# GLA and pooling trunk: one block for projection, attention and mixing, the last gates in another buffer, W_out's first part after tile 1's

## The chip, the core and the metric

The kernel runs on one core of one Trainium2 chip. The metric is the device time of one execution in microseconds (us), median of several runs. The core has five engines with instruction streams of their own: PE (TensorE: matmuls into PSUM banks), ACT (ScalarE), DVE (VectorE), POOL (GpSimd) and SP (SyncE, which here issues nearly all DMAs). They order each other by semaphores: an instruction raises one when it is done, another waits for a value. Sixteen DMA engines move data between HBM and SBUF.

## What is computed

Two layers over x of shape (1, 2048, 1024), all in float32. The first is a gated linear attention in chunks of 64 rows with 4 heads:

```python
h = x @ w_in
q, k, v, g, lr = split(h)
gk = log_sigmoid(lr @ w_gk + b_gk) / 16
bcum = cumsum(gk, within chunk)
qe, ke, kd = q * exp(bcum), k * exp(-bcum), k * exp(b_last - bcum)
o = tril(qe @ ke.T) @ v + qe @ S_prev       # S: state carried from chunk to chunk
o = rmsnorm(o) * norm_w * silu(g)
x = layernorm(ALPHA * x + o @ w_out)
```

The second layer projects x to a pooled branch and a gate, takes causal means over 2, 4, 8 and 16 rows, multiplies by a matrix for each group and by the gate, projects back, and ends in the same residual and norm.

## The kernel before

Every large product is made of three PE matmuls of rounded halves (L213 to L215): an operand is copied by ACT to a rounded "hi", and DVE subtracts it from the raw value for a "lo". So each new operand costs one ACT and one DVE instruction before PE can use it.

The program has three stages. `prepare` folds weights and has its own block. `project` (L543) computes q, k, v and the gates in 24 steps of 7 products each; its instructions stand in a second block (L731), one stream for each engine. Attention (`attend_and_norm`, L1484) and mixing (`pool_mix_and_out`, L2144) share a third block (L3035). Where a block ends, all engines meet: none begins the next block before all have ended this one. After the second block POOL clears the semaphores of the projection (L1479), whose numbers the mixing uses again.

Some work of attention is already written into the end of the projection's streams: the scores, outputs and key-value product of tile 0 on PE (`first_scores`, `first_outputs`, `first_kv`), tile 0's hi and lo parts, and on SP the loads of tile 0 and tile 1 and the first two of four loads of W_out (1 MB each). The last things that each engine does in the projection's block are: PE tile 0's key-value product; ACT `last_silu` and the copies of the last turned keys (`copy_keys`, L1162) into `kn_last`; DVE the decays of tiles and `norm_of` the last gates (L1422); SP four stores of these gates (`store_gates`, L793), each after `norm_of`.

Attention works on 16 tiles of 128 rows. In the third block SP first stores `kn_last` (two DMAs, L1694), loads W_out's last two parts (L1697), the gates g of tiles 0 and 1, x of tile 0, and then in step 0 q, k2, kn and v of tile 2 (L189), the norm's parameters and x of tile 1. Each step t of the other engines:

- ACT (L1917): the rounded sum, Ln and Exp for the RMS norm of tile t-1, the rounded gated output, then `kv_parts` of tile t+1 (L1865: kn_hi and v_hi, which wait for all four loads of that tile), then the square of tile t's output. In steps 0 to 2 parts of W_out (`w_parts`, L1873, 16 in all, each 128x512) are spread between these: part 0 ahead of `kv_parts` in step 0, parts 1 and 2 behind it, 3 and 4 at the step's end; in step 1 parts 5 to 7 behind `kv_parts` and 8 to 11 at the end. Part n needs W_out's load (n mod 8) // 2.
- DVE (L2088): masks of the scores, W_out's part 0 in step 0 (L2093), `advance` (the state: a copy in step 0), the gated product of tile t-1 (two multiplications, the second by the loaded g), o_lo, `kv_parts` of tile t+1 (L2045: q times the decay, kn_lo, v_lo), further parts of W_out, the sums of squares, the residual of tile t-2. In step 0 DVE waits ahead of `kv_parts` of tile 1 until the gates are stored (L2048), since the buffer of v_lo of tile 1 overlaps that of the last gates, `g_main` (L589).
- PE (L1821): scores of tile t; after the state and `kv_parts` the key-value product of the tile (12 matmuls of 128x256); the product with W_out of tile t-2 (from step 2 on, 24 matmuls of 128x512 in each half, with the two matmuls of the RMS mean after the first six); the outputs of tile t.

Of the kernel before, what the change touches and what calls it, by code (L numbers as in the profile page):

```python
# [4 lines left out]
F32 = mybir.dt.float32  # L5
F32R = mybir.dt.float32r
I32 = mybir.dt.int32
ALU = mybir.AluOpType
# [3 lines left out]
P = 128  # L12
# [530 lines left out]
def project(nc, p, a, last_copy, last_store, ahead):  # L543
# [44 lines left out]
    g_at = p.at = p.w_end  # L588
    g_main = p.place("h_g_main", [P, 4, BLK])  # L589
# [4 lines left out]
    chunk_end = p.place("h_chunk_end", [P, HALF_CHUNKS])  # L594
    assert p.at <= SBUF_END
# [17 lines left out]
    held = []  # L613

    def sem(name):
        held.append(nc.alloc_semaphore("h_" + name))
        return held[-1]

# [6 lines left out]
    (columns, w_summed, x_hi_done, x_lo_done, product_mm, seeded, p5_copied, u2_copied, c11_copied, c21_copied,  # L625
     u3_added, c12_added, rows_loaded, x_turned, x_copied, x_stored, x_summed, terms_stored, rank_loaded, rank_hi, rank_lo, rank_mm,
     rank_rounded, rank_ready, gk_loaded, gk_hi, gk_lo, gk_mm, ln_done, chain, scanned, ends_read, q_exp, exps_ready, q_done,
     turned, kn_copied, silu, normed) = (
        sem(n) for n in (
            "columns", "w_summed", "x_hi_done", "x_lo_done", "product_mm", "seeded", "p5_copied",  # L630
            "u2_copied", "c11_copied", "c21_copied", "u3_added", "c12_added", "rows_loaded", "x_turned", "x_copied", "x_stored", "x_summed", "terms_stored",
            "rank_loaded", "rank_hi", "rank_lo", "rank_mm", "rank_rounded", "rank_ready", "gk_loaded", "gk_hi", "gk_lo",
            "gk_mm", "ln_done", "chain", "scanned", "ends_read", "q_exp", "exps_ready", "q_done", "turned", "kn_copied",
            "silu", "normed"))
# [96 lines left out]
    with nc.Block() as block:  # L731

        @block.sync
        def _(sp):
            def load_pair(i):

                if i < V_STEPS:
                    p.load_x_pair(sp, raws[i % 2], i)
                    return
                for b in range(2):  # L740
                    sp.dma_start(raws[i % 2][:, b * KT:(b + 1) * KT, :], w_src[:, :, column(i, b):column(i, b) + P]
                                 ).then_inc(pair_loaded[i % 2], DMA)

            def load_x(e, n):

                sp.wait_ge(product_mm, 7 * (e * EPOCH - 1) + n + 1)
                sp.dma_start(x_raw[ORDER[n]][:], p.x_in[e - 1, (0, 1, 3, 7, 4, 5, 6)[ORDER[n] - 1]]
                             ).then_inc(x_loaded[n], DMA)

            def load_gk(m):  # L750

                h = m % HEADS
                if m:
                    sp.wait_ge(gk_lo, m)
                for r in range(RANK_ROWS // GATE_RANK):
                    sp.dma_start(w_gk_raw[r * GATE_RANK:(r + 1) * GATE_RANK, :],
                                 a["gla_w_gk"][0][:, h * DK:(h + 1) * DK]).then_inc(gk_loaded, DMA)

            def load_rows(u):

                if u > KT:
                    sp.wait_ge(x_turned, u - KT)
                first = p.x_tile(u) * P
                sp.dma_start(rows[:], a["x"][0][first:first + P, :]).then_inc(rows_loaded, DMA)

            def store_x(u):

                sp.wait_ge(x_copied, u - KT + 1)
                half, c, b = u // KT, u % KT // 2, u % 2
                sp.dma_start(p.x_in[half, 2 * b:2 * b + 2, :, c, :].rearrange("q p n -> p q n"),  # L770
                             x_out[:].rearrange("p (q k) t -> p q (k t)", q=2)).then_inc(x_stored, DMA)

            def store_x_terms(i):
                sp.wait_ge(x_summed, 4 * (i + 1))
                sp.dma_start(p.x_in[i // HALF_K, 4:8, :, i % HALF_K, :].rearrange("q p n -> p q n"), terms[:]
                             ).then_inc(terms_stored, DMA)

            def store_v(i, b):
                if b:
                    sp.wait_ge(u3_added, i + 1)  # L780
                    sp.wait_ge(c21_copied, i + 1)
                else:
                    sp.wait_ge(c11_copied, i + 1)
                    sp.wait_ge(c12_added, i + 1)
                sp.dma_start(p.v_tiles[p.x_tile(2 * i + b)], v_out[i % 2][:, b, :]).then_inc(v_stored[i % 2], DMA)

            def store(scratch, m, col, n, src, stored):

                first = (m // HEADS * 2 + n) * HALF_K
                sp.dma_start(scratch[first:first + HALF_K, :, col * P:(col + 1) * P].rearrange("t p c -> p t c"),  # L790
                             src.rearrange("p (t c) -> p t c", c=P)).then_inc(stored, DMA)

            def store_gates(m):  # L793
                for j in range(2):
                    sp.wait_ge(normed, 2 * m + j + 1)
                    for n in range(2):
                        store(p.g_tiles, m, m % HEADS * 2 + j, n, gates(m)[:, 2 * j + n, :],
                              g_stored[ALT if m % HEADS == 0 else MAIN])

            def store_q(m):  # L800
                for n in range(2):
                    sp.wait_ge(q_done, 2 * m + n + 1)
                    store(p.q_tiles, m, m % HEADS, n, e_q[:, n * BLK:(n + 1) * BLK], q_stored)

            def store_k(m, n):
                sp.wait_ge(k_done[n], m + 1)
                store(p.k2_tiles, m, m % HEADS, n, k2_of(m)[:, n, :], k_stored)

            def store_kn(m):
                for n in range(2):  # L810
                    sp.wait_ge(kn_copied, 2 * m + n + 1)
                    store(p.kn_tiles, m, m % HEADS, n, kn_of(m)[:, n, :], kn_stored)

            def load_columns():
                with nc.allow_non_contiguous_dma(reason="small parameter vectors as columns"):
                    for dst, src in ((p.b_gk, a["gla_b_gk"][0].rearrange("(h d) -> d h", d=P)),
                                     (p.norm_w, a["gla_norm_w"][0].rearrange("(j d) -> d j", d=P)),
                                     (p.b_grp, a["pool_b_grp"][0].rearrange("g (m d) -> d (g m)", d=P)),
                                     (p.scale, a["pool_scale"][0].rearrange("(m d) -> d m", d=P))):
                        sp.dma_start(dst[:], src).then_inc(columns, DMA)  # L820

            load_rows(KT)
            last_store(sp)
            for s in range(2):
                sp.wait_ge(p.x_in_stored[s], NT // 4 * DMA)
            load_pair(1)
            load_gk(0)
            with nc.allow_non_contiguous_dma(reason="16 columns of the gates' first factor"):
                sp.dma_start(rank_raw[:], w_src[:, :, 2 * KD + 2 * VD:2 * KD + 2 * VD + GATE_RANK]
                             ).then_inc(rank_loaded, DMA)  # L830
            for i in range(STEPS):
                e = i // EPOCH + 1
                for n in range(-1, PRODUCTS - 1):
                    if n == -1 and 1 <= i <= V_STEPS:
                        store_v(i - 1, 1)
                    if n == -1 and i and i % EPOCH == 0:
                        load_x(e - 1, PRODUCTS - 1)
                    if n >= 0 and i % EPOCH == EPOCH - 1 and i + 1 < STEPS:
                        if n == 0:
                            sp.wait_ge(terms_stored, HALF_K * e * DMA)  # L840
                        load_x(e, n)
                    if n == 0 and i + 2 < STEPS:
                        sp.wait_ge(w_lo_done, parts_to(i, PRODUCTS - 1))
                        sp.wait_ge(w_hi_done, PRODUCTS * (i + 1))
                        if i:
                            sp.wait_ge(w_summed, 4 * i)
                        if i < V_STEPS:
                            sp.wait_ge(x_summed, 4 * (i + 1))
                        if HALF_K <= i + 2 < V_STEPS:
                            sp.wait_ge(x_stored, 2 * (i + 3 - HALF_K) * DMA)  # L850
                        load_pair(i + 2)
                    if i == 0 and n == 0:
                        store_x_terms(0)
                    if i < HALF_K and n in (2, 5):
                        u = KT + 2 * i + n // 5
                        if u + 1 < NT:
                            load_rows(u + 1)
                        if n == 2:
                            store_x(u)
                    if 1 <= i <= HALF_K and n == -1:  # L860
                        store_x(KT + 2 * i - 1)
# [2215 lines left out]
```

## Time and profile before

| | |
|---|---|
| median of 3 runs | 1888.73 us (1887.55 to 1889.65) |
| the profiled execution's own time | 1888.95 us |
| its span, first to last instruction | 1887.4 us |
| mean granted clock of PE | 0.993 |
| PE / PEld / DVE / ACT / POOL busy | 97% / 80% / 72% / 45% / 35% |
| DMA | 342.83 MB, mean 182 GB/s |

The page gives shares over the whole span, in which stages with different limits are mixed. What the change touches lies between 615 and 675 us of the span, so the rows further down come from that stretch: what each engine does there, what ended its idle time, when DMAs land, how busy the DMA engines are and which clock PE was granted. Times in the rows are us from the start of the span. Weight loads overlap matmuls, so matmuls of 128x512 that take 0.39 us each start 0.23 us apart.

### The profile page before, as it was taken

The numbers are of one execution on the slowest core, as the hardware profiler recorded it, in microseconds if no ns is written. First come the engines' busy times: TensorE is split into PE (matmuls) and PEld (weight loads), VectorE is DVE, ScalarE is ACT, GpSimd is POOL, SyncE is SP. The second block draws the span as 40 slices with busy tenths as digits, with TensorE's granted clock in tenths as the row PEclk, the third lists the DMA queues.
The fourth block names the chain that finished last, engine by engine and source line by source line (L and its number), as shares of the span: only waits on it lengthen the run. The fifth ranks groups of instructions, "written<-read, shape, count | busy, mean of one in ns | idle before, by whom it ended". The sixth has DMA issues, their size and how long they took to land.

```text
span 1887.4 us, 24159 instructions
## 1 busy us (share of the span) xinstructions
PE 1840.1 (97%) x8554; PEld 1510.0 (80%) x8554; DVE 1365.1 (72%) x1647; ACT 848.7 (45%) x1308; POOL 659.1 (35%) x460
## 2 busy tenths in 40 slices
PE   9999999999999799999989999999999999999997
PEld 8878886888788688888768888878888887887885
DVE  3565566667666688787786768668899978447997
ACT  4554335656555544444444444354343444224231
POOL 0432232323231000244445655315576634223330
PEclk9999999999999899999999999999999999999998
DMA  9967764438344854675734443243456436647542
GB/s 308 317 214 247 220 208 162 124 100 292 79 136 115 310 168 150 215 250 195 264 120 133 157 148 134 98 156 123 157 187 203 148 121 234 234 145 267 179 145 101
DMA packets 256068, 342.83 MB, mean 182 GB/s; under 512 B 19024, under 2 KB 184656, under 8 KB 251344
## 3 DMA queue, kind: packets, MB, share of 16 engines
q1 hardware_dynamic: 253264, 333.97, 53.0%
q0 software_dynamic: 2688, 7.34, 1.2%
q8 instruction: 68, 1.11, 0.2%
q14 instruction: 48, 0.39, 0.1%
HBM read 221.73 MB, written 119.54 MB: 181 GB/s over the span
## 4 chain that ended last, share of the span: by engine, by line
PE 56%; DVE 5%; issue 2%; DMA 1%; ACT 1%; POOL 1%; SPq 0%; DVEq 0%; ACTq 0%; POOLq 0%
PE banks L215 17%; PE banks L213 17%; PE banks L214 17%; PE banks L1813 1%; PE banks L1817 1%; DVE m_w_lo L2799 1%; DVE m_x_lo L2813 1%; PE banks L2582 1%; DMA v<-v_tiles 1%; DMA m_ahead<-x_terms 1%; PE banks L1611 0%; PE banks L2542 0%; ACT m_x_hi L2619 0%; DVE a_stats L2040 0%; PE banks L1804 0%
## 5 line engine op out<-in xcount | busy, mean ns | idle before, releaser
L213 PE MATMUL banks<-m_x_hi,m_w_hi 128*128 128x512 f32 x1312 | 515.2, 393 | 10.2 <-DVE m_z L2874 4.4
L215 PE MATMUL banks<-m_x_hi,m_w_lo 128*128 128x512 f32 x1312 | 513.8, 392 | 0.0
L214 PE MATMUL banks<-m_x_lo,m_w_hi 128*128 128x512 f32 x1312 | 513.2, 391 | 0.0
L213 PEld LDWEIGHTS banks<-m_x_hi,m_w_hi 128*128 128x128 f32 x1312 | 247.0, 188 | 66.7 <-issue 8.3
L214 PEld LDWEIGHTS banks<-m_x_lo,m_w_hi 128*128 128x128 f32 x1312 | 246.9, 188 | 53.2 <-issue 0.7
L215 PEld LDWEIGHTS banks<-m_x_hi,m_w_lo 128*128 128x128 f32 x1312 | 246.7, 188 | 52.2
L213 PE MATMUL banks<-b_hi,h_w_hi 128*128 128x512 f32 x656 | 258.1, 393 | 4.0 <-issue 3.0
L214 PE MATMUL banks<-b_lo,h_w_hi 128*128 128x512 f32 x656 | 256.5, 391 | 0.0
L215 PE MATMUL banks<-b_hi,h_w_lo 128*128 128x512 f32 x656 | 256.4, 391 | 0.0
L2606 ACT ACTIVATE m_w_hi<-m_s 128x512 fp32r<-128x512 f32 x182 | 114.4, 629 | 204.1 <-PE banks L215 176.3
L2799 DVE TENSOR_TENSOR m_w_lo<-m_s,m_w_hi 128x512 fp32r<-128x512 f32 x182 | 161.2, 890 | 31.4 <-ACT m_w_hi L2606 30.3
L213 PEld LDWEIGHTS banks<-b_hi,h_w_hi 128*128 128x128 f32 x656 | 123.6, 188 | 31.2 <-issue 5.8
L215 PEld LDWEIGHTS banks<-b_hi,h_w_lo 128*128 128x128 f32 x656 | 123.6, 188 | 25.8
L214 PEld LDWEIGHTS banks<-b_lo,h_w_hi 128*128 128x128 f32 x656 | 123.7, 189 | 25.1
L1290 DVE TENSOR_TENSOR h_w_lo<-h_s,h_w_hi 128x512 fp32r<-128x512 f32 x93 | 70.2, 757 | 66.9 <-ACT h_w_hi L1023 66.0
L213 PE MATMUL banks<-a_w_hi,a_o_hi 128*128 128x512 f32 x256 | 101.6, 397 | 0.4 <-DVE a_res L2037 0.4
L215 PE MATMUL banks<-a_w_hi,a_o_lo 128*128 128x512 f32 x256 | 100.1, 391 | 0.0
L214 PE MATMUL banks<-a_w_lo,a_o_hi 128*128 128x512 f32 x256 | 100.0, 391 | 0.0
L1978 POOL TENSOR_TENSOR m_stage_t<-m_stage_b,m_stage_a 128x256 f32<-128x256 f32 x8 | 6.0, 747 | 257.3 <-ACT m_stage_b L1908 257.3
L2751 POOL TENSOR_TENSOR m_s<-pair_raw 128x512 f32<-128x512 f32 x24 | 45.6, 1901 | 127.2 <-PE banks L2582 81.1
L1023 ACT ACTIVATE h_w_hi<-h_s 128x512 fp32r<-128x512 f32 x93 | 58.3, 628 | 56.1 <-PE banks L215 50.3
L2799 DVE TENSOR_TENSOR m_w_lo<-m_pair_raw,m_w_hi 128x512 fp32r<-128x512 f32 x69 | 64.4, 934 | 24.7 <-ACT m_w_hi L2606 24.4
(281 smaller groups left out, 3365.3 us busy)
## 6 DMA issues: line engine op xcount, KB each, us to landing
b_raw<-x_in SPq DMA_DIRECT2D x14, 1024.0 KB, 10.6
m_x_raw<-x_terms SPq DMA_DIRECT2D x9, 1024.0 KB, 8.4
p_in<-in_pool_w_in SPq DMA_DIRECT2D x32, 256.0 KB, 5.2
w_fused<-p_out SPq DMA_DIRECT2D x32, 256.0 KB, 3.6
x_in<-h_terms SPq DMA_DIRECT2D x8, 1024.0 KB, 4.3
v_tiles<-h_v_out SPq DMA_DIRECT2D x16, 512.0 KB, 5.0
in_raw<-in_gla_w_in SPq DMA_DIRECT2D x16, 512.0 KB, 6.1
h_raw<-in_gla_w_in SPq DMA_DIRECT2D x16, 512.0 KB, 6.0
```

The costliest lines, as they stand in the source:

```text
L213: nc.tensor.matmul(out, a_hi, b_hi, start=first, stop=False, skip_group_check=True)
L214: nc.tensor.matmul(out, a_hi, b_lo, start=False, stop=False, skip_group_check=True)
L215: return nc.tensor.matmul(out, a_lo, b_hi, start=False, stop=last, skip_group_check=True)
L1023: nc.scalar.activation(parts[ORDER[n]][:], weights(i, ORDER[n]), ACT.Copy).then_inc(w_hi_done, 1)
L1290: nc.vector.tensor_tensor(w_lo[j][:], weights(i, j), w_hi[j][:].bitcast(F32), ALU.subtract).then_inc(w_lo_done, 1)
L1813: nc.tensor.matmul(o_ps[:, j * P:(j + 1) * P], v[s][:, j * P:(j + 1) * P], scores[s][:, h * P:(h + 1) * P], start=j == 4 * b, stop=False, ...
L1817: last = nc.tensor.matmul(o_ps[:, j * P:(j + 1) * P], state[s][:, j * P:(j + 1) * P], q[s][:, j // 2, P:2 * P], start=False, stop=True, sk ...
L2582: last = nc.tensor.matmul(bank(i, j), weights(set_of(i), j)[:, k, :], x_raw[j][:, k, :], start=opens and k == 0, stop=k == HALF_K - 1, ski ...
L2606: nc.scalar.activation(w_hi[ORDER[n]][:], weights(s, ORDER[n]), ACT.Copy).then_inc(w_hi_done, 1)
L2751: nc.gpsimd.tensor_tensor(s3[:], a11, a21, ALU.subtract).then_inc(w_summed, 1)
L2799: nc.vector.tensor_tensor(w_lo[j][:], weights(s, j), w_hi[j][:].bitcast(F32), ALU.subtract).then_inc(w_lo_done, 1)
L2813: nc.vector.tensor_tensor(x_lo[j][:], loaded(e, n), x_hi[j][:].bitcast(F32), ALU.subtract).then_inc(x_lo_done, 1)
```

## The change

The projection's streams become functions like those of attention and mixing, and `kernel` calls them at the head of the third block; the second block and POOL's clearing of semaphores are gone. Since all semaphores now live at once, some are shared by projection and mixing (`x_loaded`, `p5_copied`, `u2_copied`, and `ln_loaded` by attention and mixing), whose waits add what the earlier stage has counted. SP waits for the copies of `kn_last` before it stores them, which the meeting had ordered. `g_main` moves to the place of the staging buffers of step 8 and later, so DVE's wait on the stored gates goes. In step 0 DVE does `kv_parts` of tile 1 ahead of `advance` and of all parts of W_out, and ACT ahead of part 0, which both now do later in the step. Without the indentation, and without the renamed semaphores:

```diff
-def project(nc, p, a, last_copy, last_store, ahead):
+def project(nc, p, a, phase, last_copy, last_store, ahead):
...
-    g_at = p.at = p.w_end
-    g_main = p.place("h_g_main", [P, 4, BLK])
+    p.at = p.w_end
     u2 = p.place("h_u2", [P, BLK])
...
     chunk_end = p.place("h_chunk_end", [P, HALF_CHUNKS])
+    assert p.at <= p.rows_at + 2 * D * 4
+    g_at = p.at = p.rows_at + 2 * D * 4
+    g_main = p.place("h_g_main", [P, 4, BLK])
...
-    with nc.Block() as block:
-
-        @block.sync
-        def _(sp):
+    def sync(sp):
...
-    for s in held:
-        nc.gpsimd.sem_clear(s)
-        nc.release_semaphore(s)
+
+    return sync, tensor, scalar, gpsimd, vector
...
         for n in range(2):
             first, col = (2 + n) * HALF_K, HEADS - 1
+            sp.wait_ge(p.kn_copied, 2 * (2 * HEADS - 1) + n + 1)
             sp.dma_start(p.kn_tiles[first:first + HALF_K, :, col * P:(col + 1) * P].rearrange("t p c -> p t c"),
...
-            w_parts(t, {0: (0, 1), 2: (12, 16)})
+            w_parts(t, {2: (12, 16)})
             if has_next(t):
                 kv_parts(t + 1, 1 - s, pair + s, lag + 1)
-            w_parts(t, {0: (1, 3), 1: (5, 8)})
+            w_parts(t, {1: (5, 8)})
...
-            w_parts(t, {0: (3, 5), 1: (8, 12)})
+            w_parts(t, {0: (0, 5), 1: (8, 12)})
...
         def kv_parts(t, s):
 
-            if isinstance(t, int) and t == 1:
-                dve.wait_ge(p.g_stored[0], 6 * 4 * DMA)
...
-            w_parts(t, {0: (0, 1)})
+            if first(t):
+                kv_parts(1, 1)
...
-            if has_next(t):
+            if has_next(t) and not first(t):
                 kv_parts(t + 1, 1 - s)
...
-            w_parts(t, {0: (1, 3)})
+            w_parts(t, {0: (0, 3)})
...
             with nc.Block() as block:
 
                 @block.sync
                 def _(sp):
+                    produce[0](sp)
                     mix[0](sp, *attend[0](sp, load_first, load_second))
```

The other four streams get their `produce` call in the same way.

## Rows read from the trace of the kernel before

**Rows 1.** The page: busy us of each engine, share of the span, instructions.

```profile
PE 1840.1 (97%) x8554; PEld 1510.0 (80%) x8554; DVE 1365.1 (72%) x1647; ACT 848.7 (45%) x1308; POOL 659.1 (35%) x460
```

**Rows 2.** Timeline of PE: start, duration, line, [idle before, what ended it].

```profile
630.84 1.13 PE L1611 MATMUL banks<-q,k 128*128 128x128 f32 x8 [0.48 <-PEq L731]
637.01 0.55 PE L213 MATMUL banks<-a_v_hi,a_kn_hi 128*128 128x256 f32 x1 [5.05 <-DVE a_v_lo L2054]
...
643.55 1.32 PE L1813 MATMUL banks<-a_scores,v 128*128 128x128 f32 x8 [2.79 <-DVE a_gated L2013]
...
651.21 0.35 PE L213 MATMUL banks<-a_v_hi,a_kn_hi 128*128 128x256 f32 x1 [1.32 <-DVE a_v_lo L2054]
...
654.96 0.47 PE L1761 MATMUL banks<-a_sum_hi,mean_w 128*128 128x512 f32 x1 [0.71 <-issue]
```

**Rows 3.** Timeline of ACT.

```profile
626.83 1.09 ACT L1169 ACTIVATE h_kn_last<-banks 128x512 f32<-128x512 f32 x2
630.65 1.28 ACT L1910 ACT_TABLE_LOAD   x1 [2.73 <-PEq L731]
...
633.00 1.04 ACT L1871 ACTIVATE a_v_hi<-v 128x1024 fp32r<-128x1024 f32 x1
```

**Rows 4.** Timeline of DVE.

```profile
626.97 1.42 DVE L1428 TENSOR_SCALAR h_g_main<-h_g_main,norm_w 128x1024 f32<-128x1024 f32 x2 [1.55 <-ACT h_g_main L1203]
...
632.70 0.69 DVE L2063 TENSOR_TENSOR a_w_lo<-a_w_raw,a_w_hi 128x512 fp32r<-128x512 f32 x1 [4.32 <-ACT a_w_hi L1879]
...
635.65 1.22 DVE L2054 TENSOR_TENSOR a_v_lo<-v,a_v_hi 128x1024 fp32r<-128x1024 f32 x1
...
643.44 1.23 DVE L2018 TENSOR_TENSOR a_gated<-a_gated,a_g 128x1024 f32<-128x1024 f32 x1
```

**Rows 5.** The chain in order of time: start, duration, what.

```profile
637.54 10.41 DMA v<-v_tiles
647.97 0.64 ACT a_kn_hi L1870
```

**Rows 6.** DMA issues by narrow windows: KB, us to landing; at 623.6, 631.9, 633.7, 637.5.

```profile
v<-v_tiles SPq DMA_DIRECT2D x1, 512.0 KB, 4.7
...
a_w_raw<-in_gla_w_out SPq DMA_DIRECT2D x1, 1024.0 KB, 6.1
...
a_g<-g_tiles SPq DMA_DIRECT2D x1, 512.0 KB, 8.2
...
v<-v_tiles SPq DMA_DIRECT2D x1, 512.0 KB, 10.4
```

**Rows 7.** Windows: us, PE, PEld, DVE, ACT, POOL busy, PE clock, DMA share, GB/s.

```profile
628.00:629.00 1.00, 1.00 (x11) 1.00 (x10) 0.39 (x1) 0.00 (x0) 0.00 (x0) 1.00 0.32 89
629.00:630.00 1.00, 1.00 (x11) 1.00 (x10) 0.00 (x0) 0.00 (x0) 0.00 (x0) 1.00 1.00 279
...
634.00:635.00 1.00, 0.00 (x0) 0.00 (x0) 1.00 (x2) 1.00 (x4) 0.00 (x0) 0.56 0.87 194
635.00:636.00 1.00, 0.00 (x0) 0.00 (x0) 1.00 (x3) 0.99 (x2) 0.00 (x0) 0.50 1.02 401
...
656.00:658.00 2.00, 2.00 (x10) 1.65 (x9) 1.56 (x4) 1.43 (x3) 0.00 (x0) 1.00 0.05 17
```

**Rows 8.** Timeline of SP's issues of DMAs.

```profile
627.75 2.30 SPq L790 DMA_DIRECT2D g_tiles<-h_g_main  x4
630.64 1.24 SPq L1694 DMA_DIRECT2D kn_tiles<-h_kn_last  x2
631.93 1.71 SPq L204 DMA_DIRECT2D a_w_raw<-in_gla_w_out  x2
```

**Rows 9.** Timeline of PE after another pause, later in the kernel.

```profile
954.51 0.47 PE L213 MATMUL banks<-m_x_hi,m_w_hi 128*128 128x512 f32 x1 [4.44 <-DVE m_z L2874]
...
955.12 0.63 PE L215 MATMUL banks<-m_x_hi,m_w_lo 128*128 128x512 f32 x1
...
958.10 0.53 PE L213 MATMUL banks<-m_x_hi,m_w_hi 128*128 128x512 f32 x1
```

More of the change, by code:

```diff
@@ L612, in project @@
     p.g_main, p.kn_last = g_main, kn_last
[L613 to L617, printed above, removed]
+    sem = lambda name: phase.enter_context(nc.semaphore("h_" + name))
     pair_loaded, g_stored = p.in_loaded, p.g_stored
@@ new lines, in gpsimd, with sums_read, weight_sums @@
+    def gpsimd(pool):
+        def sums_read(i, j):
+            if native(i - 1, POS[j]):
+                pool.wait_ge(w_hi_done, PRODUCTS * (i - 1) + POS[j] + 1)
+            else:
+                pool.wait_ge(w_lo_done, parts_to(i - 1, POS[j]))
+        def weight_sums(i):
+            a11, a12, a21, a22 = weights(i, 1), weights(i, 2), second_row(i), weights(i, 4)
+            pool.wait_ge(pair_loaded[i % 2], 2 * (i // 2 + 1) * DMA)
+            sums_read(i, 5)
+            nc.gpsimd.tensor_tensor(s1[:], a21, a22, ALU.add).then_inc(w_summed, 1)
+            pool.wait_ge(w_summed, 4 * (i - 1) + 1)
+            sums_read(i, 6)
+            nc.gpsimd.tensor_tensor(s2[:], s1[:], a11, ALU.subtract).then_inc(w_summed, 1)
+            sums_read(i, 7)
+            nc.gpsimd.tensor_tensor(s3[:], a11, a21, ALU.subtract).then_inc(w_summed, 1)
+            sums_read(i, 3)
+            pool.wait_ge(w_summed, 4 * (i - 1) + 2)
+            nc.gpsimd.tensor_tensor(s4[:], a12, s2[:], ALU.subtract).then_inc(w_summed, 1)
+        for i in range(1, STEPS):
+            weight_sums(i)
@@ L2235, in pool_mix_and_out @@
     (w_summed, w_hi_done, w_lo_done, product_mm,
[L2236 removed]
+     seeded, c11_copied, u3_added, c12_added, silu_n1, silu_n2, chain, padded, pooled, mixed,
      stage_turned, stage_copied, stage_sum, stage_stored, x_hi_done, x_lo_done, out_added, stats_done, moments_done,
[L2238 removed]
+     rstd_done, normed_mid, normed, out_rows_loaded, out_summed, out_terms_stored) = (
         sem(n) for n in (
[L2240 removed]
+            "w_summed", "w_hi_done", "w_lo_done", "product_mm", "seeded", "c11_copied", "u3_added",
             "c12_added", "silu_n1", "silu_n2", "chain", "padded", "pooled", "mixed", "stage_turned", "stage_copied",
             "stage_sum", "stage_stored", "x_hi_done", "x_lo_done", "out_added", "stats_done", "moments_done", "rstd_done",
[L2243 to L2244 removed]
+            "normed_mid", "normed", "out_rows_loaded", "out_summed", "out_terms_stored"))
+    p5_copied, u2_copied, x_loaded, ln_loaded = p.p5_copied, p.u2_copied, p.x_loaded, p.ln_loaded
+    STEPS_BEFORE, TURNS_BEFORE, NORMS_BEFORE = 3 * (NT // 2), 2, 1
     res_loaded, out_stored = ([sem(f"{n}{s}") for s in range(4)] for n in ("res_loaded", "out_stored"))
@@ L2555, in free @@
             elif j == 7:
-                pe.wait_ge(*((u2_copied, i + 1) if i < MIX else added(i, 2)))
+                pe.wait_ge(*((u2_copied, STEPS_BEFORE + i + 1) if i < MIX else added(i, 2)))
             elif j == 3:
-                pe.wait_ge(*((p5_copied, i + 1) if i < MIX else added(i, 1)))
+                pe.wait_ge(*((p5_copied, STEPS_BEFORE + i + 1) if i < MIX else added(i, 1)))
             elif j == 4:
@@ L2566, in operands @@
                 pe.wait_ge(*weights_ready(s, j))
-                pe.wait_ge(x_loaded[n], (e + 1) * DMA)
+                pe.wait_ge(x_loaded[n], (TURNS_BEFORE + e + 1) * DMA)
                 return
@@ L2615, in turn_hi @@
             j = ORDER[n]
-            act.wait_ge(x_loaded[n], (e + 1) * DMA)
+            act.wait_ge(x_loaded[n], (TURNS_BEFORE + e + 1) * DMA)
             if e:
@@ L2916, in norm_end @@
             n, r = 2 * (o - SECOND) + b, res[res_at(o)][:, b, :]
-            dve.wait_ge(ln_loaded, 2 * DMA)
+            dve.wait_ge(ln_loaded, 2 * (NORMS_BEFORE + 1) * DMA)
             dve.wait_ge(moments_done, n + 1)
@@ L3032, in gla_pool_trunk @@
             attend, ahead = attend_and_norm(nc, p, a, phase)
-            project(nc, p, a, *prepare(nc, p, a), ahead)
+            produce = project(nc, p, a, phase, *prepare(nc, p, a), ahead)
             load_first, load_second, *mix = pool_mix_and_out(nc, p, a, out_dram, phase)
@@ L3042, in _ @@
                 def _(pe):
+                    produce[1](pe)
                     mix[1](pe, *attend[1](pe))
@@ L3050, in _ @@
                 def _(pool):
+                    produce[3](pool)
                     attend[3](pool)
```

1274 lines of the change are left out of this document (624 added, 650 removed).

## Prediction

> **What bounds the kernel now.** The page first: PE is busy for 97% of the span [rows 1]. So a change is worth only what it takes out of PE's idle time, or out of a stretch where something else sets the pace. The change touches one such stretch, some 20 us around the end of the projection, so I read that stretch engine by engine.
>
> PE first [rows 2]. It works without a gap up to the key-value product of tile 0, idles 0.48 for the meeting, does the scores of tile 1, and then idles 5.05 us until DVE has tile 1's v_lo. Later it idles 2.79, 1.32 and 0.71. These are the prizes. ACT and DVE say why the 5.05 exist [rows 3, 4]: ACT is done with the projection at 626.83 + 1.09 = 627.92 and DVE at 626.97 + 1.42 = 628.39, but both begin attention behind the meeting, ACT with a table load at 630.65 and DVE with a part of W_out at 632.70; tile 1's keys and values come after those.
>
> Then the chain in order of time, which tells what I would have missed by looking at engines alone [rows 5]. For 10.41 us, up to 648, it is no engine's work but the load of tile 2's v. ACT starts tile 2 when that load lands, and PE's product of tile 2 at 651.21 follows through DVE's v_lo [rows 2]. From there on PE has little idle time, and the change alters no order in that part. So the question of this change is one number: when does tile 2's v land?
>
> Is that load late because SP issues it late, or because the DMA engines are full? By the landings, W_out's third part takes 6.1 us, the first gates 8.2, tile 2's v 10.4, while tile 1's v, issued alone at 623.6, took 4.7 [rows 6]. The later in SP's order, the longer the wait: a queue that grows. The windows agree: the DMA share is 0.32 at 628, then about 1.0 in each microsecond, with one dip to 0.87 at 634, until it falls to 0.05 after 656 [rows 7]. So the stretch from 629 to 648 is bound by the bytes in flight, in SP's order: 1 MB of gates stored, 0.5 of keys, 2 of W_out, 1 of gates, 0.5 of x, 0.75 of q, k2 and kn, 0.5 of v, together 6.25 MB or 6.55 million bytes, in 19 us: 345 GB/s.
>
> **The change part by part.**
>
> *The meeting goes.* PE gains 0.48; ACT can start 630.65 - 627.92 = 2.7 us earlier, DVE 632.70 - 628.39 = 4.3 [rows 2 to 4]. SP ended its last stores of gates at 627.75 + 2.30 = 630.05 and went on at 630.64: it gains 0.59 [rows 8]. Its new wait (both halves of the last kn copied) is on ACT's copies that end at 627.92 [rows 3], 2 us before SP gets there, so it costs nothing; behind it in SP's order stand the stores of kn, W_out's last parts and all loads of tile 2, so a late copy would delay them one for one. POOL has no work here.
>
> *The gates' other buffer* changes where 1 MB is read from, not when, and lets DVE drop its wait on the stored gates. That wait ended nothing before: DVE's work from 632.70 to v_lo at 635.65 has no gap. With tile 1 moved up it would have bound, since the stores are issued until 630.05 [rows 4, 8].
>
> *Tile 1 ahead of W_out.* New times, from the durations above. ACT: 627.92, table load 1.28 gives 629.2, kn_hi 0.6 gives 629.8, v_hi 1.04 gives 630.8; tile 1's v has landed at 623.6 + 4.7 = 628.3 [rows 3, 5, 6]. DVE: q and kn_lo 0.6 each from 629.8, v_lo 1.2 to 632.2, then the copy of the state, as large as v_lo, to 633.4 [rows 4]. PE needs both, so tile 1's product starts at 633.4 instead of 637.01: 3.6 us earlier. Next is W_out: the moved part 0 (one of 16 on each of two engines, 0.6 and 0.7 us) changes places with tile 1's parts and is hidden by the waits that follow. But ACT's part 4 needs W_out's third load, 631.93 + 6.1 = 638.0 by its issue and landing, and the gates of tile 0 land at 633.7 + 8.2 = 641.9, where DVE used them at 643.44 [rows 4, 6, 8]. So of the 3.6 us DVE's gated product keeps 1.5. After it ACT and DVE stand at tile 2's v, which their program order puts ahead of W_out's parts 5 to 7, so these can't fill the gap.
>
> *What is late next* is thus tile 2's v. SP comes to it 0.59 us earlier at most: one end is -0.59. The other end is 0: the queue holds the same bytes in the same order, and a queue that is never empty lands its last byte at the same time. A loss is excluded on this term, since nothing new stands ahead of that load. The row at 634 tells between the ends: the DMA engines were idle for 0.13 us there, and moved 194 GB/s where the next microsecond had 401, so between a tenth and half of a microsecond was lost where SP's stores end and W_out's loads begin [rows 7]. An earlier SP closes this hole and no more. I take -0.3.
>
> *PE's clock.* The 5.05 us of idle brought the granted clock down: 0.56 at 634, 0.50 at 635 [rows 7]. Before tile 2's product at 651.21 PE idled only 1.32 us, behind 6.3 us of work (outputs of tile 1 from 643.55, 5.4 us at a slow pace, then scores), and that product ran at full pace [rows 2]. With the change the outputs start at about 641 (W_out's part 4, two short ACT steps and DVE's first gated product after 638.0) and are over by 646.5; then PE waits for tile 2's v, does 0.9 us of scores at 647.7 and waits 2.3 more. Little work and much idle, and then the stretch where PE is full. What does the trace say of the price? After 4.44 us of idle at 954.51, seven products started between 955.12 and 958.10, 0.43 apart; at the usual 0.23 they would have taken 1.4 us less [rows 9]. The bounds here: 0 if the clock stays up; at most half clock all the way to the mean of tile 2, which is twelve 128x256 products (0.1 each), six 128x512 and the two of the mean (0.2 each by rows 9), 2.8 us, of which PE's wait of 0.71 before that mean covers a part [rows 2]: +2.1. I take +0.6, nearest to the fall of rows 9: 1.4 less the 0.71. The Trainium skill, "TensorE: Matmul & The Clock Gate", section "HAM oscillation — how this bites in real kernels", says that a wait for DMA between tiles lets the clock gate throttle again, so that each next tile starts slow. The trace bears this out in part: the pauses of 5.05 and 4.44 us were followed by half clock, that of 1.32 was not. Where it held in full, the time would be that of the second rival below.
>
> *Sum.* Against the profiled execution's own 1888.95 (span 1887.4, the rest lies around it): -0.3 + 0.6 = +0.3. That execution is 0.2 above the median 1888.73, so about 1889.0. The 3.6 us that tile 1 wins are real, and are given back in the wait for tile 2's v.
>
> **The rivals.**
>
> *The whole wait comes back (faster).* If the 10.41 us of tile 2's v were SP's lateness and not the queue's, tile 1's gain would pass on: 3.6 us at the product and 0.48 of the meeting, up to the full 5.05, hence 1883.7 to 1884.7. For it: tile 2's v is the last of eleven issues that SP makes one after another from 630.64 on [rows 8]. Against: the share of 1.0 [rows 7], and that SP moves by 0.59 only.
>
> *PE meets tile 2 at half clock (slower).* Place: 651.21. Price: the far bound above, +2.1, with no help from the load: 1890.8. It decides when PE's idle before that product grows beyond the 1.32 that it stood and is not made up by work in between; the idle of 2.79 at 643.55 is the nearest larger one [rows 2]. To be slower by a margin that can be measured it would have to lose 3.8 + 0.7 us, some 9 us at half clock, three times the 3 us of rows 9.
>
> *It doesn't do what it says.* If DVE or ACT still stand at a wait that the meeting hid (tile 1's loads, the stored keys), tile 1 starts as late as now, and the time is that of before, 1888.7.
>
> **How the numbers follow.** Chances: forecast (tile 2's v sets the end, some clock lost) 0.74; the whole wait 0.10; half clock at tile 2 0.12; no effect 0.04. The forecast's ends, -0.59 and +1.2, with the 1 us by which the runs before spread give 1887.1 to 1890.9. Taking in the half clock, and leaving out the whole wait: 1886.9 to 1891.5. About 0.2%, 3.8 us, is what a measurement of this kernel can tell from no change. Faster by more: the whole wait, 0.10. Slower by more: the far part of the half clock, 0.05. The rest, 0.85, is within it.
>
> **What would show it.** In the changed kernel: ACT's table load near 628; PE's idle before tile 1's product shrunk from 5.05 to about 2; tile 1's v_lo at 631; a DMA share of 1.0 without the dip near 634; ACT idle before tile 2's kn_hi, released by the load of v, until 647.4 to 648; PE's product of tile 2 within 0.6 us of 651.2. The clock near 651 tells the third term. I am wrong if tile 2's v lands before 645, or if the DMA share falls below 1 between 630 and 648.

## The result, and the profile after

The changed kernel took 1890.83 us (median of 12 runs, 1889.13 to 1894.31), the kernel before, beside it, 1887.62 (12 runs, 1886.61 to 1889.65): a ratio of 1.0019, 95% interval 1.0010 to 1.0028. Measured a second time, in another series, it took 1888.24 against 1888.00, ratio 1.0004 (0.9995 to 1.0013). So the change gives nothing, and perhaps costs a little; 1889.0 was forecast. The profiled execution took 1890.05, its span is 1888.3, and the page's busy times are those of [rows 1] but for 3.5 us at most:

```profile
PE 1839.9 (97%) x8554; PEld 1508.5 (80%) x8554; DVE 1368.6 (72%) x1647; ACT 849.2 (45%) x1308; POOL 662.1 (35%) x460
```

All stands earlier or later here by what the stages before it took. So times below are often given from the first store of the last gates, SP's first row, which is 627.75 in the kernel before [rows 8]. SP's timeline after (start, duration):

```profile
626.60 2.31 SPq L786 DMA_DIRECT2D g_tiles<-h_g_main  x4
628.96 1.78 SPq L1686 DMA_DIRECT2D kn_tiles<-h_kn_last  x2
630.78 1.72 SPq L204 DMA_DIRECT2D a_w_raw<-in_gla_w_out  x2
...
636.62 1.20 SPq L186 DMA_DIRECT2D v<-v_tiles  x1
```

SP goes on 0.05 us after the stores of the gates, where it stood 0.59 before [rows 8]; but the two stores of keys now take 1.78 to issue in place of 1.24, and at W_out SP is level again: 630.78 - 626.60 = 4.18, as 631.93 - 627.75 = 4.18 before. Tile 1 did what was forecast. ACT and DVE:

```profile
626.79 1.28 ACT L1902 ACT_TABLE_LOAD   x1
...
637.10 0.63 ACT L1871 ACTIVATE a_w_hi<-a_w_raw 128x512 fp32r<-128x512 f32 x1 [1.34 <-DMA a_w_raw<-in_gla_w_out]
...
648.23 0.63 ACT L1862 ACTIVATE a_kn_hi<-kn 128x512 fp32r<-128x512 f32 x1 [4.90 <-DMA v<-v_tiles]
```

```profile
630.06 1.22 DVE L2044 TENSOR_TENSOR a_v_lo<-v,a_v_hi 128x1024 fp32r<-128x1024 f32 x1
...
641.01 1.23 DVE L2010 TENSOR_TENSOR a_gated<-a_gated,a_g 128x1024 f32<-128x1024 f32 x1 [0.79 <-DMA a_g<-g_tiles]
...
648.89 0.69 DVE L2042 TENSOR_TENSOR q<-q,a_tile_decay 128x512 f32<-128x512 f32 x1 [4.30 <-ACT a_kn_hi L1862]
```

The table load follows the copies of the last keys at once (it waited 2.73, [rows 3]). Then the gain is spent piece by piece, each time in a wait for a load: 1.34 us for W_out's third part, 0.79 for the gates, and 4.90 for tile 2's v, where DVE waits 4.30 in its turn. PE shows the same:

```profile
632.47 0.39 PE L213 MATMUL banks<-a_v_hi,a_kn_hi 128*128 128x256 f32 x1 [2.36 <-DVE a_state L1991]
...
640.37 2.04 PE L1805 MATMUL banks<-a_scores,v 128*128 128x128 f32 x8 [5.18 <-DVE a_gated L2005]
...
648.25 1.16 PE L1602 MATMUL banks<-q,k 128*128 128x128 f32 x8 [2.04 <-DMA v<-v_tiles]
...
651.47 0.55 PE L213 MATMUL banks<-a_v_hi,a_kn_hi 128*128 128x256 f32 x1 [2.06 <-DVE a_v_lo L2044]
...
673.58 0.50 PE L1753 MATMUL banks<-a_sum_hi,mean_w 128*128 128x512 f32 x1 [0.27 <-DVE a_sum_lo L2075]
```

Tile 1's product begins 5.87 us after the gates' store (9.26 before): 3.4 earlier. Tile 2's begins 24.87 after it, 23.46 before: 1.4 later. The chain in order of time names the load between them:

```profile
636.62 11.59 DMA v<-v_tiles
648.23 0.64 ACT a_kn_hi L1862
```

11.59 us where it was 10.41 [rows 5], though the DMA share is 0.99 or more in each microsecond from 635 to the landing. Windows (the columns of [rows 7]) show this, and the clock:

```profile
634.00:635.00 1.00, 0.68 (x4) 0.30 (x2) 1.00 (x3) 1.00 (x3) 0.00 (x0) 1.00 0.86 328
635.00:636.00 1.00, 0.19 (x1) 0.00 (x0) 1.00 (x3) 0.76 (x2) 0.00 (x0) 1.00 0.99 401
...
647.00:648.00 1.00, 0.00 (x0) 0.00 (x0) 0.00 (x0) 0.00 (x0) 0.00 (x0) 1.00 1.02 410
...
652.00:653.00 1.00, 1.00 (x7) 1.00 (x6) 1.00 (x2) 0.27 (x1) 0.00 (x0) 0.50 1.08 346
```

At 647 no engine does anything at all, and the DMA engines move 410 GB/s: the stage is bound by bytes in flight. From 651.5 to 654.9 PE works at granted clock 0.50, where the kernel before had 1.00:

```profile
652.00:653.00 1.00, 1.00 (x10) 0.95 (x9) 1.00 (x3) 0.02 (x1) 0.00 (x0) 1.00 1.06 347
```

SP issues the same transfers in the same order in both kernels, so a transfer that differs must be one that SP does not issue. The list of DMA queues has it, in windows of 2 us: after at 644 to 646, ahead of v's landing at 648.2, and before at 647 to 649, around its landing at 647.95 (number of packets, MB, share of 16 engines):

```profile
q8 instruction: 1, 0.02, 3.4%
```

The row is word for word the same in both kernels; only its place differs. One packet of 16 KB fetches instructions, and 3.4% of 16 engines for 2 us is 1.09 us on one engine. It can be placed more closely: between the landing of tile 2's kn and that of its v, which SP issues next. From the issue of kn (SP's rows, before and after) and its time to landing (the same row in both):

```profile
636.65 0.84 SPq L182 DMA_DIRECT2D kn<-kn_tiles  x1
635.71 0.87 SPq L182 DMA_DIRECT2D kn<-kn_tiles  x1
kn<-kn_tiles SPq DMA_DIRECT2D x1, 256.0 KB, 10.0
```

kn has landed at 646.65 before and at 645.71 after, v 1.3 us later before and 2.5 later after. So of the 1.4 us that v comes later (from the gates' store), some 1.2 arise between these two landings, where the fetch lies; 0.2 are there already at kn.

Where these few us go between the two profiled executions, from the rows above and [rows 8]: the stages before the gates' store -1.15 (626.60 against 627.75, work that the change does not touch; in the thirteen traces of this case the place lies between 624.8 and 629.0); from there to tile 3's mean +1.58 (673.58 - 626.60 = 46.98; before, 673.15 - 627.75 = 45.40); behind it +0.47; in all the +0.9 by which the spans differ. The row of before, from its chain:

```profile
673.15 0.51 PE banks L1761
```

### The profile page after: what moved, and what is told of

The parts are those of the page before. It is cut to its first block, busy times and chain, and to the rows that moved or that the text cites. A ratio compares the mean times of both kernels' runs of the same rounds, so it can differ in the third digit from the quotient of the medians.

```text
span 1888.3 us, 24097 instructions
## 1 busy us (share of the span) xinstructions
PE 1839.9 (97%) x8554; PEld 1508.5 (80%) x8554; DVE 1368.6 (72%) x1647; ACT 849.2 (45%) x1308; POOL 662.1 (35%) x460
## 4 chain that ended last, share of the span: by engine, by line
PE 79%; DVE 5%; issue 3%; DMA 3%; ACT 2%; SPq 1%; POOL 1%; DVEq 0%; ACTq 0%; POOLq 0%
PE banks L213 24%; PE banks L215 24%; PE banks L214 24%; PE banks L1805 1%; PE banks L1809 1%; DVE m_w_lo L2791 1%; PE banks L954 1%; DVE m_x_lo L2805 1%; DMA m_x_raw<-w_terms 1%; PE banks L932 1%; ACT m_x_hi L2611 1%; DMA v<-v_tiles 1%; DMA m_ahead<-x_terms 1%; DMA b_raw<-x_in 1%; PE banks L1602 0%
## 5 line engine op out<-in xcount | busy, mean ns | idle before, releaser
L2791 DVE TENSOR_TENSOR m_w_lo<-pair_raw,m_w_hi 128x512 fp32r<-128x512 f32 x72 | 65.2, 906 | 26.0 <-ACT m_w_hi L2598 25.5
```

Source lines behind the costliest of these rows:

```text
L2791: nc.vector.tensor_tensor(w_lo[j][:], weights(s, j), w_hi[j][:].bitcast(F32), ALU.subtract).then_inc(w_lo_done, 1)
```

## The experiments

Three theories. Q: the stage ends when tile 2's v lands; what the change wins stops there, and an instruction fetch that PE, running ahead in tile 1, now brings in front of that landing makes it later still. C: PE's clock loses the time. R: what differs lies in the rest of the kernel, and from run to run. The measures, all worked out as above, in us from the first store of the last gates:

| kernel | time, beside before | v of tile 2 lands | fetch begins | mean of tile 2 | mean of tile 3 |
|---|---|---|---|---|---|
| before | | 20.20 | 19.8 | 27.21 | 45.40 |
| changed | 1890.83, 1887.62 | 21.61 | 18.5 | 29.27 | 46.98 |
| changed, again | 1888.24, 1888.00 | 21.54 | 18.2 | 29.50 | 47.21 |
| parts moved, meeting kept | 1887.65, 1888.00 | 20.11 | 20.1 | 27.12 | 45.31 |
| one block, parts not moved | 1890.36, 1888.08 | 21.52 | 18.7 | 29.20 | 46.91 |
| outputs held | 1888.18, 1888.08 | 20.50 | 24.7 | 28.35 | 46.06 |
| waits for PE | 1892.98, 1888.00 | 21.76 | 19.4 | 28.78 | 46.97 |
| three products | 1889.33, 1888.08 | 22.15 | 18.8 | 29.16 | 47.35 |
| tile 2 first | 1883.77, 1888.00 | 14.01 | 17.4 | 23.19 | 41.16 |
| tile 2 first, meeting kept | 1885.71, 1888.08 | 13.85 | 19.6 | 25.48 | 43.66 |
| tile 2 first, again | 1883.89, 1888.35 | 13.84 | 17.3 | 22.77 | 40.95 |

**The changed kernel again**, with no edit.

> The changed kernel once more, for a second trace and a second set of times. Theory Q (the DMA queue and the instruction fetch in it set tile 2's start): the load of tile 2's v lands again 21 to 22 us after the first store of the last gates (20.2 before, 21.6 in the first trace of the changed kernel), with an instruction-fetch DMA between 640 and 648 us; the loss up to the PE product of tile 2 is again 1 to 2 us, and the time is 2 to 4 us above the kernel before. Theory C (PE's clock is the loss): the product of tile 2 starts as early as before against the gates' stores, and the loss stands in slow products after it, other in each trace. Theory R (the loss is spread over the mixing): the two kernels differ by more behind 700 us than ahead of it.

Ratio 1.0004 (0.9995 to 1.0013). The landing at 21.54 and tile 3's mean at 47.21 repeat the first trace: the stage loses 1.6 to 1.8 us, 0.09% of the kernel, each time; of the 2 to 4 us that were expected in the time, 0.2 came. The rest of the first measurement's 0.19% did not repeat. Behind tile 3's mean the two traces are 0.5 us longer and 0.5 shorter than before: what theory R looks at is scatter in these traces, and shows no loss of the change.

**Parts moved, meeting kept.** The kernel before with the other buffer and tile 1 ahead of W_out, but two blocks:

```diff
-    g_at = p.at = p.w_end
-    g_main = p.place("h_g_main", [P, 4, BLK])
+    p.at = p.w_end
...
+    g_at = p.at = p.rows_at + 2 * D * 4
+    g_main = p.place("h_g_main", [P, 4, BLK])
...
-            w_parts(t, {0: (0, 1)})
+            if first(t):
+                kv_parts(1, 1)
```

> The kernel before with its two blocks and the meeting, but with the gates in the other buffer and tile 1's parts ahead of W_out's: one part of the change alone. Theory Q: tile 2's v comes as in the kernel before, so the time is that of before within 1 us (1887 to 1889), and the fetch of instructions lies as in before. Theory C: PE's idle before tile 2 grows as in the changed kernel, since tile 1 starts 1 to 2 us earlier, and 1 to 3 us are lost: 1889 to 1891. Theory R: as before.

Ratio 1.0001 (0.9992 to 1.0010), v at 20.11. Moving the parts alone costs nothing and wins nothing. Its chain row:

```profile
635.05 10.40 DMA v<-v_tiles
```

**One block, parts not moved.** The changed kernel with the parts of tile 1 behind W_out's part 0, as before:

```diff
-            if first(t):
-                kv_parts(1, 1)
+            w_parts(t, {0: (0, 1)})
...
-            if has_next(t) and not first(t):
+            if has_next(t):
                 kv_parts(t + 1, 1 - s)
```

> The changed kernel with W_out's part 0 ahead of tile 1 again and the state's copy ahead of tile 1's parts: the one block and the other buffer alone. Theory Q: tile 1 still starts some 3 us earlier than before and PE runs ahead of the fetch's old place, so v lands 21.3 to 21.7 us after the first store of the gates and the time is that of the changed kernel within 1 us, 1888 to 1889.5. If the moved parts were the cause of the loss: v lands at 20.2 and the time is that of before.

Ratio 1.0010 (1.0001 to 1.0019). v lands at 21.52 and the load takes 11.32 us: the loss of the load is there in full without the moved parts (the time, 1890.36, is 0.9 above what was expected). It comes with the meeting's end, and so does PE's running ahead: the fetch begins at 18.7, as in the changed kernel.

```profile
635.10 11.32 DMA v<-v_tiles
```

**Outputs held.** If the fetch is the cause, v must land early again when PE reaches that place later. PE's second half of tile 1's outputs waits until tile 2's four loads have landed; no DMA that the kernel issues is touched.

```diff
-        def outputs(s):
+        def outputs(s, hold=False):
...
             for b in range(2):
+                if hold and b:
+                    pe.wait_ge(in_loaded[1 - s], 2 * p.QKV_LOADS * DMA)
...
-                outputs(s)
+                outputs(s, isinstance(t, int) and t == 1)
```

> The changed kernel, but PE does the second half of tile 1's outputs only when tile 2's four loads have landed. PE then comes later to the place in its stream at which the next 16 KB of its instructions are fetched (18.1 and 18.5 us after the first store of the gates in the two traces of the changed kernel, ahead of tile 2's v). Theory Q with the fetch as the cause: the fetch comes after that landing, v lands 20.1 to 20.5 us after the first store of the gates instead of 21.5 to 21.6, and the time falls by 1 to 2 us against the changed kernel; PE's 1.8 us of held outputs and 0.9 of scores fit into the 3.2 us that ACT and DVE need after the landing. If the fetch isn't the cause: v lands at 21.5 to 21.6 again and the time stays or grows by up to 1 us.

The fetch begins at 24.7, behind the landing, and v lands at 20.50, 1.2 us behind kn, its load again as long as before:

```profile
634.88 10.44 DMA v<-v_tiles
```

Of the 1.3 to 1.4 us, 1.1 are back, by an edit to PE alone. This is the run that shows Q's second half. Ratio 1.0008 (0.9999 to 1.0017): what the load gives back, the held products spend in part, so tile 3's mean gains only 0.9 to 46.06, and the 1 to 2 us expected in the time do not show (1888.18; the changed kernel 1890.83 and 1888.24).

**Waits for PE.** Meant to move the fetch by other means, some 200 waits that are long met, spread over PE's products in the projection, so that its instruction blocks fall elsewhere:

```diff
             last.then_inc(product_mm, 1)
+            for _ in range(2 if i < 5 else 1):
+                pe.wait_ge(w_hi_done, 1)
```

> The changed kernel with some 200 waits that are already met, added behind products of the projection on PE, so that the fetches of PE's instructions (16 KB each, about 256 instructions apart) fall elsewhere: no longer between 628 and 648 us while the DMA engines are full, but near 623 and 651. Theory Q with the fetch as the cause: tile 2's v lands about 1.2 us earlier against the gates' stores (20.2 to 20.5 us after the first), and the time falls by 1 to 2 us, to 1889. If the fetch isn't the cause: it lands as before, 21.6 us after, and the time stays. The waits themselves cost under 1 us.

Only 61 of them became instructions of their own, and the fetch moved from 18.5 to 19.4, still 2.3 us ahead of the landing at 21.76, so the run does not do what it was meant to. The kernel was slower, 1.0029 (1.0019 to 1.0038), by something outside the stage that stays open. But its trace shows which measure to trust. The load of v took 10.44 us here, just as without a fetch ahead of it, but SP issued it 1.3 later (11.33 us after the gates' store, against 10.01), so the length of a load alone doesn't tell what delayed it. The time from kn's landing to v's does: it is 1.9 here, 1.8 to 2.5 in all five traces with the fetch well ahead of v's landing (the two of the changed kernel, one block, waits for PE, three products), and 1.2 to 1.3 in the other eight.

**Three products.** Theory C by itself: three products of 128x512 that nobody reads, on PE, two behind tile 1's outputs and one behind tile 2's scores, to keep the clock up.

```diff
+        def filler(count):
+            for _ in range(count):
+                nc.tensor.matmul(y_ps[0], p.ident[:], p.mask[:].rearrange("p h c -> p (h c)"), start=True, stop=True)
...
                 scores_of(s)
+                if isinstance(t, int) and t == LAG:
+                    filler(1)
...
                 outputs(s)
+                if isinstance(t, int) and t == 1:
+                    filler(2)
```

> The changed kernel with three 128x512 products of constants on PE whose result nobody reads: two behind the outputs of tile 1, one behind the scores of tile 2, to keep PE at work while it waits for tile 2's v. Theory C: the clock stays at 1.00 from 648 to 655, tile 2's product runs at its full pace, and the mean of tile 2 starts 0.4 to 0.8 us earlier against the gates' stores (28.5 to 28.9 us after the first instead of 29.3 to 29.5). Under both theories v lands where it did, 21.5 us after, and the time falls by at most 0.8 us, within what can be told from no change.

The clock stayed up at tile 2 (the windows of this kernel; the changed one had 0.50):

```profile
652.00:653.00 1.00, 1.00 (x11) 1.00 (x10) 1.00 (x2) 0.27 (x1) 0.00 (x0) 1.00 1.09 390
```

From v's landing to tile 2's mean it took 7.01 us, as in the kernel before (27.21 - 20.20 = 7.01); the changed one took 29.27 - 21.61 = 7.66, and 7.96 the second time. So the clock costs 0.65 to 0.95 there. But in this trace v landed 0.5 later, and tile 3's mean is no earlier; the ratio is 1.0010 (1.0001 to 1.0019). The clock's price is shown; that removing it speeds the kernel up is not.

**Tile 2 first.** Q's first half. SP issues W_out's third part, the gates of tile 0 and then all of tile 2, and only then W_out's last part, the keys' stores, the gates of tile 1 and x: 2.5 MB less ahead of v.

```diff
+        p.load_out_rows(sp, 2)
+        load_g(0, 0)
+        sp.wait_ge(o_mm, 1)
+        p.load_qkv(sp, 2, 0)
+        p.load_out_rows(sp, 3)
         for n in range(2):
...
-        for n in (2, 3):
-            p.load_out_rows(sp, n)
-        load_g(0, 0)
...
-            if not (static and t + 2 >= NT):
+            if not (static and (t == 0 or t + 2 >= NT)):
```

> The changed kernel with SP's order altered: W_out's third part, the gates of tile 0, then tile 2's q, k2, kn and v, and only then W_out's fourth part, the stores of the last kn, the gates of tile 1 and x. 2.5 MB that stood ahead of tile 2's v go behind it. Theory Q: tile 2's v lands 5 to 7 us earlier, at about 641 to 643, the PE product of tile 2 starts at 645 to 647 instead of 651.5, and the time falls by 3.5 to 6 us against the changed kernel, to 1885 to 1887, below the kernel before. Rival (SP's issues or the engines' own work hold tile 2): no change beyond 1 us. Theory C: at most 1 us of gain.

v lands at 14.01, 7.6 us earlier than in the changed kernel and 6.2 earlier than before; the fetch, at 17.4, is now behind it, so 1.1 to 1.4 of the 7.6 are the fetch's and not the order's. Tile 3's mean is 5.8 earlier than in the changed kernel and 4.2 earlier than before, and the time follows, somewhat below the 1885 to 1887 expected: 1883.77, ratio 0.9979 (0.9970 to 0.9988). It beats both kernels. ACT no longer waits for v at all:

```profile
643.17 1.06 ACT L1929 ACTIVATE a_o_hi<-a_gated 128x1024 fp32r<-128x1024 f32 x1 [3.17 <-DVE a_gated L2012]
644.13 0.61 ACT L1864 ACTIVATE a_kn_hi<-kn 128x512 fp32r<-128x512 f32 x1
```

**Tile 2 first, meeting kept.** The same edit to the kernel before.

> The kernel before, two blocks and the meeting, with SP's order altered as in the run that put tile 2's loads ahead. Theory Q: with tile 2's v out of the way, tile 1's late start sets the end; the time falls against before by 0.5 to 2.5 us, to 1885.5 to 1887.5, and stays 1.5 to 3.6 us above the same order in the one block (1883.8), which is what the meeting costs when nothing else hides it. Rival (the meeting costs nothing even then): the time is that of the one block, 1883 to 1884.5.

1885.71, ratio 0.9985 (0.9976 to 0.9994). So of the 4.2 us, some 2.4 come from the order of loads alone, and 1.9 by the medians from the change that was predicted to be worth nothing: one block and moved parts together, which were not taken apart here. By time alone that second share is not certain, since the two intervals overlap; at tile 3's mean it is 2.5, and 2.7 in the repetition below (43.66 against 41.16 and 40.95). Without the queue behind it, the change pays.

**Tile 2 first, again, and two edits to it.** What bounds that version? PE does tile 1's outputs at half clock there, and DVE stands close behind.

> The version with tile 2's loads ahead, a second time, beside the next two. Theory K (PE's clock now sets tile 2): in its first trace PE idled 4.47 us before tile 1's outputs and did them at granted clock 0.50, so that tile 2's product began 20.3 us after the first store of the gates, though DVE had v_lo ready at 18.8. Theory D (DVE sets it): the clock costs nothing, since the rest of tile 2 waits for DVE anyway. Both expect the same here: 1883.3 to 1884.3, mean of tile 3 41.0 to 41.5 us after the first store of the gates.

> The version with tile 2's loads ahead, and eight products of 128x512 into a free bank on PE behind the RMS mean of tile 1, in the 4.47 us that it idles there (a result that nobody reads). Theory K: the granted clock stays up, tile 1's outputs take 3.6 us in place of 6.5, and tile 2's product waits for v_lo alone: 18.9 us after the first store of the gates in place of 20.3, the mean of tile 3 1.4 us earlier, time 1882.2 to 1882.9. Theory D: the product is earlier, but the mean of tile 3 stays at 41 us and the time at 1883.8.

> As the run with eight products on PE, and in step 1 ACT's and DVE's parts of tile 2 ahead of the hi and lo parts of tile 1's gated output, whose keys and values have landed at 14.0 us after the first store of the gates while ACT idles to 14.2. Worked out from the first trace: v_lo is ready at about 17.7 in place of 18.8, the lo part of the gated output as v_lo before at 18.8, and tile 2's product begins at 17.7. Theory K, with the clock up: 1.2 us more than the run with eight products alone, 1881.0 to 1881.8. Theory D: the first half of W_out waits for the lo part of the gated output and DVE's parts of W_out, so that the mean of tile 3 gains less than 0.5, within 0.5 us of the run with eight products.

```diff
                 mean(t, c)
+                if isinstance(t, int) and t == 1:
+                    filler(8)
```

```diff
+            if isinstance(t, int) and t == 1:
+                kv_parts(t + 1, 1 - s)
             if has(t, lag, 1):
                 dve.wait_ge(o_hi_done, t)
```

(the second diff is DVE's, without the line that leaves tile 2's parts out further down, and ACT's is alike; the third kernel has both). The three took 1883.89, 1884.40 and 1884.18, ratios 0.9978 (0.9968 to 0.9987), 0.9984 (0.9975 to 0.9993) and 0.9979 (0.9970 to 0.9988): no difference that shows. With eight products the clock stayed at 1.00 all through, but the expectation had taken them at the pace of rounded products, 0.23 us each; of plain float32 they took 0.88:

```profile
635.06 7.03 PE L1804 MATMUL banks<-mask,ident 128*128 128x512 f32 x16
641.92 1.05 PE L1811 MATMUL banks<-a_scores,v 128*128 128x128 f32 x8
```

So the outputs begin at 641.92, 2.4 us after the end of DVE's first gated product (638.35 + 1.21 = 639.56), which they wait for otherwise, and tile 2's product comes at 19.67 and 19.68 us, not at 18.9 and 17.7, against 19.01 without them. Yet tile 2's mean begins at 22.76 or 22.77 and tile 3's at 40.95 in all three, for DVE's last step before tile 2's mean comes at the same time whatever PE does. In the run with eight products:

```profile
645.43 1.89 DVE L2061 TENSOR_TENSOR a_w_lo<-a_w_raw,a_w_hi 128x512 fp32r<-128x512 f32 x3
647.24 0.68 DVE L2080 TENSOR_TENSOR a_square_sum<-a_square 128x512 f32<-128x512 f32 x1
648.61 0.69 DVE L2083 TENSOR_TENSOR a_sum_lo<-a_square_sum,a_sum_hi 128x512 fp32r<-128x512 f32 x1 [0.70 <-ACT a_sum_hi L1915]
```

The sum is ready for PE 21.97 us + 0.69 after the gates' store in each of the three, behind a DVE whose only gap from 636 on is this 0.70, in which ACT rounds the sum. Theory K falls and D holds for that mean in these three: the next bound is DVE, with ACT's one step in its chain. It is a near thing: in the first trace of this version tile 2's product came at 20.32, and the mean at 23.19, with no pause of PE before it, so there PE set it, 0.4 later, of which tile 3's mean kept 0.2. An edit that takes work off DVE was not run.

## Why the prediction was right and where it was not

**What bounds the stage: right.** Tile 2's v was named as the number that decides, and the queue of bytes as its cause. Taking 2.5 MB from in front of it moved v by 6.35 us with the meeting kept (20.20 to 13.85) and the time by 2.4; in the changed kernel, with the fetch, v by 7.6 and the time by more than 4. The first rival, that the wait was SP's lateness, is out: SP stood level at W_out, and the wait grew.

**Tile 1: right.** 3.6 us earlier forecast, 3.4 measured; of it 1.5 was to be left at DVE's gated product, and 1.3 was (641.01 - 626.60 = 14.41 against 15.69, [rows 4]); and all of it was gone at tile 2's v. Waits of 2.36 before tile 1's product ("about 2") and of 2.06 before tile 2's ("2.3 more") were as said. Tile 2's product came at 651.47, "within 0.6 us of 651.2", but that is luck: the whole stretch began 1.15 us earlier in this trace, and from the gates' store the product is 1.4 late.

**Tile 2's load: wrong, and with the wrong sign.** Forecast -0.3 between -0.59 and 0, measured +1.4 (+1.3 again). The step that failed is "A loss is excluded on this term, since nothing new stands ahead of that load". It counted what SP issues. PE's own instruction fetch is also a DMA: it had begun 0.4 us before v landed, which did no harm that shows, and PE, 3 us ahead in tile 1, brought it to 3.1 us before. In twelve of thirteen traces it begins with 6066 to 6098 of PE's instructions begun (matmuls, weight loads and its sequencer's); with the added waits it is at 6127, later by about their number. So it goes with PE's place in its program, not with time. That the fetch is enough to delay the landing is shown by the held outputs, and where it does so by the 1.8 to 2.5 us from kn's landing to v's in place of 1.3. That it does so because v needs all 16 engines and one of them is taken for 1.09 us is argued: no row names the engine of a packet. The 0.2 by which kn was late already in the first trace have no known cause; in the second trace the fetch began 1.6 us ahead of kn's landing too, and kn itself was 0.9 late. Nor was the -0.3 there to be had: one of the prediction's own signs of being wrong, a DMA share below 1 between 630 and 648, came, since the dip at 634 stayed (0.87 before [rows 7], 0.86 after) though SP no longer waited there; SP, whose two stores of keys took 0.54 longer to issue, was level again at W_out, and with the fetch out of the way v landed at 20.50, not before 20.20.

The Trainium skill, "Runtime: NRT & Kernel Launch", section "Instruction fetch mechanics", says that an engine's sequencer fetches its next 16 KB block of 256 instructions by a DMA queue of its own while it works on, and that the cost of crossing into the next block is mostly hidden. The traces bear out the block (0.02 MB in one packet) and that PE is not held up by it (busy for all of 645 to 646, where the fetch begins); hidden it is not here, since it is someone else's load that pays.

**PE's clock: right in size where it falls, less at the end.** +0.6 forecast; 0.65 to 0.95 at tile 2's mean. Tile 3's mean kept 0.2 to 0.5 of it (from v's landing 46.98 - 21.61 = 25.37 and 47.21 - 21.54 = 25.67, before 45.40 - 20.20 = 25.20), as PE's pause before it shrank from 0.69 to 0.27, a wait that the forecast did not count.

**The sum.** +0.3 forecast from two terms, +1.58 and +1.81 measured at tile 3's mean: the load's term was off by 1.6 to 1.7 and the clock's, there, by -0.1 to -0.4. The forecast of 1889.0 lies between the two measurements, 1890.83 and 1888.24, and no effect beyond 0.2% was the likeliest class; but that the median came close owes as much to the scatter of the whole kernel as to the sum: 1.6 us is 0.09%, inside the second interval and just below the first. What made the first measurement 0.19% is not known. The second rival, half clock at tile 2, is what happened in kind (0.50 from 651.5 to 654.9), at a third to a half of its +2.1: the clock was back at 1.00 before the mean, where the rival had it at half all the way.

## What to carry to other kernels

Where a load is late, ask first how many bytes stand in front of it: moving 2.5 MB that nobody yet needed behind it was worth 2.4 us alone and seems to have made another 1.9 us of the change count, while an earlier start of the engines alone was worth nothing. In a stage with full DMA engines, count every kind of packet, the instruction fetches too, which move when an engine runs ahead. And an edit worth nothing may become worth something when the bound next to it goes, so it should be tried again then.

## What the runs showed of the hardware

- An instruction fetch of 16 KB went as one packet, took 1.09 us in the full queue and, ahead of a 512 KB load, came with a landing 1.1 to 1.4 us later than where the fetch lay behind it.
- In this kernel pauses of PE were followed by half clock even when broken up: 2.04 us idle, about 1.2 of scores and 2.06 idle, and then 0.50 from 651.5 on; with three products in these pauses it stayed at 1.00. A single pause of 1.32 [rows 2] was not followed by it.
- A product of 128x512 took 0.88 us with plain float32 operands at granted clock 1.00, where the rounded ones start 0.23 apart: the trace shows 16 matmuls for eight products.
- SP's time to issue the two stores of keys was 1.78 us where it followed the stores of the gates at once, against 1.24 behind the meeting, so the 0.54 that SP won there were gone at W_out.
